# Token mixing of an RWKV stage: three key tiles block by block, a new order of units and mixes, and half of the mixes' first parts on GpSimd

## What is computed

```python
xx = jnp.pad(h, ((0, 0), (1, 0), (0, 0)))[:, :T] - h
xr, xw, xk, xv, xa, xg = (h + xx * mu[i] for i in range(6))
r = xr @ w_r
k = xk @ w_k
v = xv @ w_v
logw = -jax.nn.softplus(-(w0 + jnp.tanh(xw @ w1) @ w2)) - 0.5
a = jax.nn.sigmoid(a0 + (xa @ a1) @ a2)
g = jax.nn.sigmoid(xg @ g1) @ g2
```

## Time and profile before

| | us |
|---|---|
| three runs | 2595.59, 2596.20, 2596.39 (median 2596.2) |
| the profiled execution, own time | 2603.86 |
| its span | 2602.1 |
| PE busy | 2510.2 (96%) |
| DVE busy | 1336.2 (51%) |
| ACT busy | 1123.0 (43%) |
| GpSimd busy | 995.2 (38%) |
| the first stage, up to the last mix | 0 to about 101 |

### The profile page before, as it was taken

The page is one execution under the profiler, slowest core; times in us unless marked ns, Lnnn a source line. Parts: engine busy times, 40 slices in busy tenths (PEclk is TensorE's granted clock), DMA queues, the critical chain, the costliest instruction groups (busy, mean ns, idle before and its releaser), DMA issues.

```text
span 2602.1 us, 62231 instructions
## 1 busy us (share of the span) xinstructions
PE 2510.2 (96%) x25266; PEld 2370.8 (91%) x25266; DVE 1336.2 (51%) x2034; ACT 1123.0 (43%) x1653; POOL 995.2 (38%) x488
## 2 busy tenths in 40 slices
PE   7999898999999999998999999999999999999998
PEld 6888886997999999977989999999998769999998
DVE  7666564513477741798523677622153344455521
ACT  8844445544433432425534344433245444444422
POOL 3333220562344444325423444444443104444442
PEclk9899999999999999999999999999999999999999
DMA  4221001351223233323222332233222103223232
GB/s 153 76 67 50 1 1 63 99 177 41 90 97 97 97 98 107 121 65 113 82 65 65 97 97 91 96 106 120 83 95 68 47 1 97 97 89 97 96 99 74
DMA packets 62180, 219.43 MB, mean 84 GB/s; under 512 B 6752, under 2 KB 9184, under 8 KB 61408
## 3 DMA queue, kind: packets, MB, share of 16 engines
q1 hardware_dynamic: 58880, 207.76, 24.8%
q10 hardware_dynamic: 3168, 9.75, 1.0%
HBM read 213.29 MB, written 4.19 MB: 84 GB/s over the span
## 4 chain that ended last, share of the span: by engine, by line
PE 83%; DVE 8%; issue 6%; ACT 2%; POOL 1%; DMA 0%; DVEq 0%; POOLq 0%; ACTq 0%
PE psum L571 70%; DVE psum L2698 5%; PE psum L713 3%; PE psum L721 2%; PE psum L1072 1%; PE psum L1021 1%; PE psum L1251 1%; PE psum L1290 1%; POOL wl L520 1%; DVE psum L2269 1%; ACT wh L1382 0%; PE psum L1253 0%; PE psum L683 0%; PE psum L1060 0%; PE psum L1278 0%
## 5 line engine op out<-in xcount | busy, mean ns | idle before, releaser
L520 POOL TENSOR_TENSOR wl<-raw,wh 128x1024 fp32r<-128x1024 f32 x388 | 949.1, 2455 | 1461.8 <-ACT wh L1382 1461.7
L571 PE MATMUL psum<-acth,wh 128*128 128x256 f32 x3792 | 763.4, 283 | 18.3 <-DVE actl L2789 8.0
L571 PE MATMUL psum<-actl,wh 128*128 128x256 f32 x3792 | 752.8, 280 | 0.0
L571 PE MATMUL psum<-acth,wl 128*128 128x256 f32 x3792 | 752.4, 280 | 0.0
L1382 ACT ACTIVATE wh<-raw 128x1024 fp32r<-128x1024 f32 x388 | 407.1, 1056 | 624.0 <-PE psum L571 600.5
L571 PEld LDWEIGHTS psum<-acth,wh 128*128 128x128 f32 x3792 | 582.4, 189 | 35.8 <-issue 28.1
L571 PEld LDWEIGHTS psum<-actl,wh 128*128 128x128 f32 x3792 | 581.6, 189 | 0.0
L571 PEld LDWEIGHTS psum<-acth,wl 128*128 128x128 f32 x3792 | 581.1, 189 | 0.0
L2628 DVE TENSOR_TENSOR cu<-psum,rstd 128x512 f32<-128x512 f32 x132 | 91.0, 690 | 237.8 <-PE psum L571 220.6
L571 PE MATMUL psum<-hidh,wh 128*128 128x256 f32 x1056 | 209.5, 276 | 0.0
L571 PE MATMUL psum<-hidl,wh 128*128 128x256 f32 x1056 | 209.3, 276 | 0.0
(11 more groups left out here) (443 smaller groups left out, 4056.0 us busy)
## 6 DMA issues: line engine op xcount, KB each, us to landing
raw<-in_weights SPq DMA_DIRECT2D x388, 512.0 KB, 3.4
xt<-in_x SPq DMA_DIRECT2D x4, 512.0 KB, 5.5
xt<-in_x ACTq DMA_DIRECT2D x1, 2048.0 KB, 9.3
out_x<-xt SPq DMA_DIRECT2D x6, 256.0 KB, 2.3
mem<-in_mem ACTq DMA_DIRECT2D x1, 1024.0 KB, 11.1
memn<-memh ACTq DMA_DIRECT2D x1, 1024.0 KB, 5.6
memn<-meml ACTq DMA_DIRECT2D x1, 1024.0 KB, 9.1
memh<-memn ACTq DMA_DIRECT2D x1, 1024.0 KB, 4.7
```

Source lines behind the costliest of these rows:

```text
L520: pool.tensor_tensor(wl[:, s, :], raw[:, s, :], wh[:, s, :].bitcast(F32), ALU.subtract).then_inc(split_done, 1)
L571: ins = pe.matmul(out[:, n:n + HALF], w, m[:, n:n + HALF], start=first and n == 0, stop=last and n + HALF >= out.shape[1])
```

## The change

- `STREAM` and PE's order become ka (3), kb (2), lora_w, kc (3), lora_a, gate_in (2). The counters of the plan follow.
- `MIXES` becomes "kwagvr": v before r. The r tiles still come before the v tiles.
- PE makes the three ka tiles together: for each block k one product of each of the three tiles, into three banks.
- Of the mixes behind the first (m from 8 on) those with odd m get their first part from GpSimd, by a tensor_scalar into `sq`, a buffer in SBUF, instead of from ACT into PSUM. That is 20 of 48. ACT's parts of the even m run three ahead of the high parts instead of two.
- GpSimd's order is written out: wl of units 0 to 3, parts 9 and 11, then for u = 4 to 12 wl of unit u followed by parts 4u-3 and 4u-1, then wl of units 13 to 15, then the loop as before.
- On ACT, weight_high(0) and weight_high(1) come earlier, and the key tiles, the narrow projections and the gate's are placed anew among the mixes. The last mixes run as v 3 to 6, gate_in 0, v 6 to 8 and r 0 to 3, gate_in 1, r 3 to 8.

```diff
-    ("ka", 3), ("lora_w", 1), ("kb", 2), ("lora_a", 1), ("kc", 3), ("gate_in", 2), ("w2a2", 1), ("r", 8), ("v", 8),
+    ("ka", 3), ("kb", 2), ("lora_w", 1), ("kc", 3), ("lora_a", 1), ("gate_in", 2), ("w2a2", 1), ("r", 8), ("v", 8),
-MIXES = "kwagrv"
+MIXES = "kwagvr"
+        def shared(m):
+            return m >= KT and m % 2 == 1
         def mixed_part(m):
-            return bank[4 + m % 2]
+            return sq[:, m // 2 % 2, :] if shared(m) else bank[4 + m % 2] if m < KT else bank[4 + m // 2 % 2]
...
+            def mix_parts(*ms):
+                for m in ms:
+                    c = m % KT + MU[MIXES[m // KT]] * KT
+                    pool.wait_ge(val_ready, plan("mixk", "val") + m - 3)
+                    pool.tensor_scalar(mixed_part(m), x(m % KT), omu[:, c:c + 1], None, ALU.mult).then_inc(odd_part, 1)
...
-            with pool.Fori(0, LOWS_FIRST) as i:
+            weight_lows(0)
+            pool.wait_ge(omu_ready, 1)
+            pool.wait_ge(h_ready, KT)
+            mix_parts(9, 11)
+            for u in range(4, 13):
+                weight_low(u // SLOTS, u % SLOTS)
+                mix_parts(4 * u - 3, 4 * u - 1)
+            for u in range(13, 16):
+                weight_low(u // SLOTS, u % SLOTS)
+            with pool.Fori(4, LOWS_FIRST) as i:
                 weight_lows(i)
...
-            for j in range(3):
-                mixed("ka", j, "k")
+            for k in range(KT):
+                part("mixk", k)
+                for j in range(3):
+                    u, t = UNIT0["ka"] + j, plan("ka", "tile") + j
+                    if k == 0:
+                        split_unit(u)
+                        free_bank(t)
+                    ins = product(bank[t % 4], u % SLOTS, k, mixh[MIX_TO["k"]][:, k, :], mixl[MIX_TO["k"]][:, k, :],
+                                  k == 0, k == KT - 1)
+                    if k == KT - 1:
+                        ins.then_inc(units_used, 1)
...
             act.activation(tmp[:, 0, 0:1], b_eps, ACT.Ln)
+            weight_high(0)
             act.wait_ge(sum_mm, plan("norm0", "total") + 1)
...
-            weight_high(0)
+            weight_high(1)
             act.wait_ge(omu_ready, 1)
             mix_part(0)
             mix_part(1)
-            weight_high(1)
...
-            mix_high("w", 0, 4)
+            mix_high("w", 0, 2)
             key_tile(0)
-            mix_high("w", 4, 6)
+            mix_high("w", 2, 3)
             key_tile(1)
-            mix_high("w", 6, 8)
+            mix_high("w", 3, 4)
             key_tile(2)
-            mix_high("a", 0, 4)
+            mix_high("w", 4, 8)
+            key_tile(3)
+            mix_high("a", 0, 2)
+            key_tile(4)
+            mix_high("a", 2, 5)
             used("lora_w")
...
-                mix_high("v", 3 if j == 0 else 6, 6 if j == 0 else 8)
+                if j == 0:
+                    mix_high("v", 6, 8)
+                    mix_high("r", 0, 3)
+                else:
+                    mix_high("r", 3, 8)
...
             def mix_value(m):
-                dve.wait_ge(part_ready, m + 1)
+                if shared(m):
+                    dve.wait_ge(odd_part, (m - KT) // 2 + 1)
+                else:
+                    dve.wait_ge(part_ready, m + 1 if m < KT else KT + (m - KT) // 2 + 1)
...
-                if m == MIXES.index("r") * KT + 1:
+                if m == MIXES.index("v") * KT + 4:
                     low_in_place(midl[:, :], mid_all[:, :], midh[:, :], "lora_a")
```

More of the change, by code:

```diff
@@ L179, in build_program @@
     plan.take("knorm", sq=KT)
-    for stage, n in (("ka", 3), ("lora_w", 1), ("kb", 2), ("lora_a", 1), ("kc", 3), ("gate_in", 2), ("w2a2", 16),
+    for stage, n in (("ka", 3), ("kb", 2), ("lora_w", 1), ("kc", 3), ("lora_a", 1), ("gate_in", 2), ("w2a2", 16),
                      ("r", 8), ("v", 8), ("g2", 8), ("o", 8)):
@@ L424, in build_program @@
         omu_ready, h_ready, part_ready = sem("omu_ready"), sem("h_ready"), sem("part_ready")
+        odd_part = sem("odd_part")
         sq_ready, sq_used = sem("sq_ready"), sem("sq_used")
@@ L516, in _, with weight_low @@
         def _(pool):
+            def weight_low(i, s):
+                pool.wait_ge(split_hi, i * SLOTS + s + 1)
+                pool.tensor_tensor(wl[:, s, :], raw[:, s, :], wh[:, s, :].bitcast(F32),
+                                   ALU.subtract).then_inc(split_done, 1)
             def weight_lows(i):
                 for s in range(SLOTS):
-                    pool.wait_ge(split_hi, i * SLOTS + s + 1)
-                    pool.tensor_tensor(wl[:, s, :], raw[:, s, :], wh[:, s, :].bitcast(F32),
-                                       ALU.subtract).then_inc(split_done, 1)
+                    weight_low(i, s)
+            def mix_parts(*ms):
[3 more added lines that the diff above has]
+                    pool.tensor_scalar(mixed_part(m), x(m % KT), omu[:, c:c + 1], None, ALU.mult).then_inc(odd_part, 1)
             def core_stage(i, c, n):
@@ L646, in mixed @@
                 tile(stage, j, "mix" + name, mixh[MIX_TO[name]], mixl[MIX_TO[name]])
[L648 to L649 removed]
+            for k in range(KT):
[9 more added lines that the diff above has]
+                        ins.then_inc(units_used, 1)
             pe.wait_ge(h_ready, KT)
[L651 removed]
             for j in range(2):
                 mixed("kb", j, "k")
[L654 removed]
+            mixed("lora_w", 0, "w")
             for j in range(3):
                 mixed("kc", j, "k")
+            mixed("lora_a", 0, "a")
             for j in range(2):
@@ L1407, in mix_part @@
                 k, c = m % KT, m % KT + MU[MIXES[m // KT]] * KT
+                if shared(m):
+                    return
                 if m < KT:
@@ L1410, in mix_part @@
                 if m >= 2:
-                    act.wait_ge(val_ready, plan("mixk", "val") + m - 1)
+                    act.wait_ge(val_ready, plan("mixk", "val") + m - (1 if m <= KT else 3))
                 act.activation(mixed_part(m), x(k), ACT.Identity, scale=omu[:, c:c + 1]).then_inc(part_ready, 1)
@@ L1419, in mix_high @@
                     act.activation(to[:, k, :], mixed_value(m), ACT.Identity).then_inc(hi_ready, 1)
-                    if m + 2 < len(MIXES) * KT:
-                        mix_part(m + 2)
+                    ahead = 2 if m < KT - 1 else 3
+                    if m + ahead < len(MIXES) * KT:
+                        mix_part(m + ahead)
             def high_part(stage, to, n=T, count=KT):
@@ L1552, in _ @@
             weight_high(UNIT0["lora_w"] + SLOTS)
[L1553 to L1557, removed]
+            mix_high("a", 5, 8)
+            key_tile(5)
+            mix_high("g", 0, 3)
+            key_tile(6)
+            mix_high("g", 3, 7)
+            key_tile(7)
+            mix_high("g", 7, 8)
+            mix_high("v", 0, 3)
             used("lora_a")
@@ L1560, in _ @@
             weight_high(UNIT0["lora_a"] + SLOTS)
[L1561 to L1566, removed]
+            mix_high("v", 3, 6)
             for j in range(2):
```

1 line of the change is left out of this document (added).

## The result

| | before | after |
|---|---|---|
| runs, median (range), us | 2595.89 (2593.49 to 2596.39, four) | 2612.95 (2609.72 to 2616.86, four) |
| ratio to before, with its 95% interval | | 1.0062 [1.0048, 1.0075] |
| the profiled execution, own time | 2603.86 | 2609.72 |
| its span | 2602.1 | 2607.9 |
| PE, DVE, ACT, GpSimd busy | 2510.2, 1336.2, 1123.0, 995.2 | 2503.9, 1348.2, 1112.2, 1026.7 |

The change costs 12.5 to 19.5 us, all of it more than the 5.2 us that I had named as the bound. The forecast was 2599.5, its range ended at 2606.0. "The mark" is used from here on for the time at which ACT starts on w2a2's banks, the line from which everything shifts as a whole. It moved by 11.97 us where I had forecast 3.3. A ratio is always that to the runs of the kernel before taken alongside, with its 95% interval in brackets; a mark is read from one profiled execution.

What follows compares the result with a forecast made beforehand. The mixes' end, paced by DVE and ACT, bounds w2a2's start: 31.95 + 58.0 + 6.2 + 3.5 + 4.2 + 0.6 = 104.5, so w2a2's emptying starts at 103.5 against 100.17, 3.3 later; 2596.2 + 3.3 = 2599.5 us, range 2593.0 to 2606.0.

Steps and rivals of the forecast that it cites:

- What bounds the stage: First stage: when the mixes end and w2a2 can run; DVE loses about 10 us to holes from ACT's insertions.
- price P: Time of one GpSimd first part, taken as 0.61 us from a copy, with 1.2 as upper end.
- part 2: Odd values reading two SBUF tensors are held by GpSimd on DVE: about 0.8 us each, 4 to 4.5 in all.
- part 1: Twenty first parts leave ACT, 12.4 us of its work; by itself a gain of 5 to 6 us.
- part 3: ACT waits 4.2 us at key tile 0, which starts at 39.5; the mixes lose 6.2 us.
- the formula: An odd DVE value behind a GpSimd part and wl is held P + 0.25, less 0.1: about 0.8 us net.
- parts 2 and 4: Part 4, last mixes: order changes nothing more; wl 13 to 15 in a row hold values 45 and 47, already counted.
- Rival (a): GpSimd's part is dear: with P = 1.2, +4.5 us, late clock +1.7; 2604 to 2606 us; chance 0.30.
- (b): DVE's holds are missing or hidden behind waits for ACT: 4.2 us less, 2595.3 us, no change; chance 0.13.
- (c): PE's clock stays up before the first tile, key tile 0's wait goes: 5 us, 2594.5; chance 0.15 with (d).
- (d): Mixes were never the bound, PE's early start carries to the end: 4.7 us won, 2591.5; chance 0.15 with (c).

Runs made afterwards that it cites:

- first experiment: The changed kernel with all 48 first parts back on ACT, nothing else changed; median 2603.72 us, ratio 1.0038.
- second experiment: The changed kernel with odd values from m = 9 reading only xt, GpSimd still making its parts; one execution, 2595.23 us.
- the other execution of after: The changed kernel, unchanged, run again in more rounds; ratio 1.0061.
- more products: Four more constant products on PE ahead of the first tile: in the changed kernel 2611.37 us, ratio 1.0035; in the kernel with free slots ratio 0.9986.
- the kernel with free slots: Before's tile order, ka block by block, ten first parts on GpSimd, ACT's insertions moved behind m = 12, 16 ... 44; median 2597.75 us, ratio 0.9995.
- the kernel with the copy: The changed kernel with GpSimd's part a copy of x, its multiplication by 1 - mu left out; one execution, 2605.81 us.
- the kernel with the offload alone: The kernel before with only the odd first parts moved to GpSimd, tile order and key tiles as they were; one execution, 2604.45 us.

## Why the prediction was wrong, by its own steps

**What bounds the stage: right.** The shift made in the mixes is carried through w2a2 (124.59 - 112.14 = 12.45 us against my 12.5) to the r tile: 11.97 at the mark, 11.94 there.

**The steps that failed: the price P in part 2, and the relief in part 1.** In each column the first three rows add up to the shift of the mark.

| us of the mark | in the sum | measured |
|---|---|---|
| part 2, the holds | +4.2 | +9.6 |
| part 1, ACT's relief | -7.1 | -1.8 |
| part 3, order, blocks and the wait at key tile 0 | +6.2 | +4.2 |
| the shift | +3.3 | +12.0 |

The sum without parts 2 and 3 puts the mark at 103.5 - 4.2 - 6.2 = 93.1, which is 7.1 ahead of 100.17; the words of part 1 say 5 to 6. The measured terms are differences between kernels, taken one after the other (first experiment, then second, then after). The 4.2 is the 3.2 of the first experiment and the 1.0 by which key tile 0 came later in this execution of after. In another order the terms would come out otherwise, since the parts of the change don't add up.

**Part 2: the mechanism held, its price failed.** A value held by a wl ends 0.55 us after it. The Trainium skill, "SBUF — State Buffer", section "SBUF: two separate sides", calls the port pair an exclusive lock, for the whole instruction, between GpSimd and a VectorE instruction with two SBUF inputs. Beside a wl this trace agrees (2.64 us instead of 0.76), and the second experiment, with one such input, has no hold at all. Beside a part it doesn't: value 19 ended 0.3 us before the part did, and value 17 wasn't held by the second half of one. So a part costs little by its own hold; it costs by putting the wl behind it over the next odd value, and that is what the formula counts. The formula, P + 0.25 less 0.1, gives 1.71 us for the measured P of 1.56; values 21, 25, 29 and 33 took 1.88, 1.68, 1.65 and 1.63 over 0.76. From 21 on the held values are those that parts 2 and 4 name; 13, 15 and 19 were held too, and 17 wasn't.

The price P was wrong. I took 0.61 from a copy, and called 1.2, half of a wl, the upper end. The true 1.56 lies above both. With it the sum gives eight holds 0.95 dearer, 7.6 us, and a mark at 111.1, against 112.14 measured. That it comes so near is luck: it has the holds at 11.8, 2.2 too much, and parts 1 and 3 together 3.3 too early. Measured, the price alone is worth 6.1 us (111.28 - 105.17, with key tile 0 at 38.91 in both). The upper end had no ground: a subtraction of two tensors bounds a multiplication of one by a value of its partition only if the input count sets the price. The Trainium skill, "GPSIMD Engine Reference", section "When to use GPSIMD", has one-input work at roughly line rate. I leaned on that; the copy at 0.61 may pass for it, the tensor_scalar at 1.56 doesn't.

**Rival (a) was the case that came,** with the direction and the condition as named (slower from P = 0.85 on), and bounded too low by the same 1.2. Its time, 2604 to 2606, falls short of 2612.95 also because part 1 was too good. It had a chance of 0.30. Its other half, the clock rising only at 31, did not come: it rose near 26.6 where I had taken 27.

**Part 3: right up to the mixes behind key tile 0.** Forecast: key tile 0 at 39.5 after a wait of 4.2, value 12 at 42.3, value 14 at 46.8. Measured: 39.71, 4.18, 42.57, 47.21. The 38.91 of the other execution of after and the 40.88 with more products lie within the bounds of 38.5 to 41.2. Its share of the end was put too high. I had 6.2 us for it. The first experiment has all of order and blocks at 3.2, with key tile 0 at 38.70: its low 12 is 5.6 us late (45.82 against 40.25), and 2.4 of that is given back by shorter holes later.

**Part 1 was too good.** I forecast 5 to 6 us from ACT's relief and put 7.1 into the sum, and it is 1.8 (second against first experiment). I had counted ACT's load as a mean, 0.79 per mix. But a hole arises at one place: the high part behind an insertion. In these runs it got shorter only where the slot beside it lost its part, which the kernel with free slots shows (2.2 us), and which the equal holes of 0.75, 1.16 and 2.17 show from the other side. Part 1 is off by 5.3 us, part 3 by 2.0 the other way, so the two errors hid each other in part.

**Rivals (b), (c), (d).** The holds were not missing (b). The clock fell (c), in both profiled executions of the changed kernel; with more products ahead it stayed up in one kernel, whose mark came 0.7 us earlier by it (98.43 against 99.10), and not in the other. PE's early start did not carry (d).

**From the mark to the end.** I forecast that the shift is the same in the runs. The ratio of the runs says 12.5 to 19.5 us, the mark 12.0. In the profiled pair the spans differ by 5.8 only. The difference goes later, in the stretches where the granted clock falls below 1.00: the shift is 12.2 us at 150 to 220, 10.6 at 290 to 400, 8.2 at 490 to 1200, 4.3 at 1380 to 2010 and 5.9 to the end. Other executions scatter in the same way: span less mark is 2501.9 and 2497.2 for two of the kernel before, 2495.8 and 2499.3 for two of after, 2490.1 to 2504.4 over all kernels. So one pair of spans can't weigh a change of 12 us here, and the mark can.

**Left open.** The medians put both after and the first experiment some 4 to 7 us higher than their marks do (16.1 against 12.0; 9.9 against 3.2). The profiled executions show no slower rest for them. That the ratio with more products of constants falls to 9 us, with two of its runs at 2603 to 2604, hints that some of it is the clock of the first tiles in executions without a profile. No run here separates it.

## What to carry to other kernels

Before work is moved to GpSimd beside a busy VectorE, ask two things of each pair of instructions: does VectorE's read two SBUF tensors, and what does GpSimd's own form cost. A VectorE operand left in PSUM removes the hold altogether, as every even value of this kernel shows. Ask too what GpSimd runs right behind the moved work, since here it was mostly that which held VectorE. A price for one form of instruction is no bound for another: where a term of the sum is multiplied by the count of its holds, leave the range open upwards until the form has a row. And taking work off an engine paid here only at the place where another waits for it: with the insertions moved into the freed slots the holes shrank, with the insertions left in place they stayed.

## What the runs showed that I had not expected

- GpSimd's tensor_scalar with a value of each partition takes 1.56 us for 128x512 in float32, 2.6 times the copy's 0.61. It is even dearer than the subtraction of two tensors of that size, which I estimate at half of the 2.41 for 128x1024.
- Yet a part holds VectorE for less than half of its 1.56 us. The values that begin within 0.3 us of a part's start (13 and 19, in all three executions of this order, and 23 of the kernel with the offload alone) end 1.23 to 1.26 us after its start. One held by a wl ends 0.55 after the wl's end, so by my estimate the part let go about 0.7 us after its start. Value 17, 0.7 into its part, takes 0.76 in all three. Why, no run here shows.
- The hold works both ways. In the kernel with the copy a wl that begins over a running odd value takes 2.87 us instead of 2.41:

```profile
44.02 2.87 POOL L524 TENSOR_TENSOR wl<-raw,wh 128x1024 fp32r<-128x1024 f32 x1
...
43.70 0.93 DVE L2313 SCALAR_TENSOR_TENSOR psum<-xt,par,sq 128x512 f32<-128x512 f32 x1
```

- With the same products, TensorE's clock falls and rises at other times from one execution to the next: granted 0.50 in 21 to 23 and 0.60 in 25 to 27 in the profiled execution of after, 0.67 and 0.98 in the other one. Key tile 0 lies 0.80 us apart in the two, and the mark 0.86.
